# A shared 16 KB buffer, earlier gathers, a four-column-group MLP, and other engines for probability copies and low parts

## The reference

```
mod = silu(c) @ w_ada + b_ada                       # shift, scale, gate, twice
u   = rmsnorm(x) * (1 + scale1) + shift1
q_a,k_a,v_a,q_b,k_cmp,v_cmp,k_sel,v_sel,k_win,v_win,g_nsa,g_a,g_b = split(u @ w_in)
o_a   = MoBA attention: own block of 256 and the 3 best earlier blocks, 8 heads
o_cmp = attention over compressed keys: segments of 32, stride 16, through
        gelu(flat @ w1 + b1) @ w2 + b2              # the small MLP, hidden width 256
o_sel = attention over the 16 best blocks of 64;  o_win = over the last 512 positions
o_b   = g0*o_cmp + g1*o_sel + g2*o_win
x = x + gate1 * ((sigmoid(g_a)*(o_a @ w_pa) + sigmoid(g_b)*(o_b @ w_pb)) @ w_out)
h = rmsnorm(x) * (1 + scale2) + shift2
a, b = split(h @ w_gu);  x = x + gate2 * ((silu(a)*b) @ w_down);  y = rmsnorm(x)
```

## Time and profile before

| what | value |
|---|---|
| median of 3 runs | 1269.82 us (1265.07 to 1272.02) |
| profiled execution | 1268.64 us, span 1266.2 us |
| mean granted TensorE clock | 0.926 |
| busy: TensorE, VectorE, ScalarE, GpSimd | 1133.7, 550.6, 511.7, 310.2 us |
| bytes moved by DMA | 219.94 MB, mean 174 GB/s |

### The profile page before, as it was taken

How to read it: one execution, slowest core, us unless ns; L and a number is a source line. 1 busy time by engine, 2 the same in 40 slices (tenths; PEclk the granted TensorE clock), 3 DMA queues, 4 the chain that set the end, 5 groups by cost and what they waited for, 6 DMA issues and landing times. The chain is left out here.

```text
span 1266.2 us, 24086 instructions
## 1 busy us (share of the span) xinstructions
PE 1133.7 (90%) x8797; PEld 952.6 (75%) x8797; DVE 550.6 (43%) x1009; ACT 511.7 (40%) x942; POOL 310.2 (25%) x112
## 2 busy tenths in 40 slices
PE   7899978759899999999898989969997799997996
PEld 3678955637686767777776868668997699997995
DVE  2400043432726354453628272636345577775004
ACT  3321231524544635454546354443542344332221
POOL 1233400001010000000000100044574176665540
PEclk9789987769999999999899999978998799998997
DMA  9788754028374564646373836394563054444201
GB/s 335 208 306 279 258 170 181 34 99 341 110 264 151 206 199 159 221 152 239 111 278 108 291 106 216 100 270 126 158 199 121 15 191 139 149 152 164 100 0 41
DMA packets 130048, 219.94 MB, mean 174 GB/s; under 512 B 19364, under 2 KB 74145, under 8 KB 125330
## 3 DMA queue, kind: packets, MB, share of 16 engines
...
## 5 line engine op out<-in xcount | busy, mean ns | idle before, releaser
L1839 POOL TENSOR_TENSOR b_slabL<-t_slab,b_slabH 128x2048 fp32r<-128x2048 f32 (+1 forms) x53 | 227.6, 4311 | 157.0 <-ACT b_slabH L1990 157.0
L1124 POOL DMA_INDIRECT t_nsa<-cache_nsa_kv,t_index x32 | 30.1, 940 | 587.7 <-ACT t_relay L1461 346.4
L104 PE MATMUL ps<-b_uH,b_slabH 128*128 128x320 f32 x480 | 152.3, 317 | 16.5 <-DVE b_uL L2088 9.0
L105 PE MATMUL ps<-b_uL,b_slabH 128*128 128x320 f32 x480 | 151.1, 315 | 0.0
L106 PE MATMUL ps<-b_uH,b_slabL 128*128 128x320 f32 x480 | 150.2, 313 | 0.0
L1990 ACT ACTIVATE b_slabH<-t_slab 128x2048 fp32r<-128x2048 f32 (+1 forms) x53 | 94.3, 1785 | 119.8 <-PE ps L106 111.1
L1233 PE MATMUL ps<-t_XT,t_slab 128*128 128x254 f32 x512 | 121.0, 391 | 0.0
L1195 PE MATMUL ps<-t_XT,t_slab 128*128 128x254 f32 x512 | 116.1, 380 | 1.4 <-ACT t_KTr L1461 0.7
L1233 PEld LDWEIGHTS ps<-t_XT,t_slab 128*128 128x128 f32 x512 | 97.9, 196 | 20.7 <-issue 8.6
L104 PEld LDWEIGHTS ps<-b_uH,b_slabH 128*128 128x128 f32 x480 | 92.4, 192 | 18.9 <-issue 16.2
L1195 PEld LDWEIGHTS ps<-t_XT,t_slab 128*128 128x128 f32 x512 | 94.8, 190 | 13.5 <-DVE t_XT L1445 2.0
...
## 6 DMA issues: line engine op xcount, KB each, us to landing
...
```

The lines of the kernel that those rows point to most:

```text
L104: pe.matmul(out, w_high, x_high, start=start, stop=False, **kw)
L105: pe.matmul(out, w_high, x_low, start=False, stop=False, **kw)
L1124: pool.indirect_dma_start(out=nsa[:, q % 2, :], out_offset=None, in_=d["cache_nsa_kv"], in_offset=bass.IndirectOffsetOnAxis(ap=t["index"][ ...
L1839: pool.tensor_tensor(slabL[:, s, 0:values], slab[:, s, 0:values], slabH[:, s, 0:values].bitcast(F32), ALU.subtract).then_inc(w_split, 1)
```

## The change

One buffer `nsa` of 16 KB per partition is allocated for the whole program. In the front it takes two slabs of w_ada, in the prompt the segments, then the first two gathers of the decode part, in the last decode turn u, and in the back part u and the gates. The first two gathers are issued in the prompt, after the segment transposes. The wait for the spill of the prompt's outputs moves into the decode part. The MLP's hidden layer is spread over four groups of 32 output rows, each with a quarter of the accumulation, and the matmuls that follow (with `fold`, a matrix with ones at every 32nd row) both transpose and add the four groups. In the prompt ScalarE makes all copies of transposed probabilities. In the back part VectorE makes the low parts, at written-out places of its list, and the first slab and u are split in halves and pairs. The core of the diff:

```diff
     rows_p, rows_s = t["rows_p"], t["rows_s"]
-    ada_slab = [slab[:, s, :] for s in range(SLOTS)] + [rows_p[:, :, :].rearrange("p i c -> p (i c)")[:, 0:SLABW],
-                                                        t["cp"][:, 0:SLABW]]
...
+def gather_segments(pool, t, d, b, q):
+    pool.indirect_dma_start(out=t["nsa"][:, q % 2, :], out_offset=None, in_=d["cache_nsa_kv"],
+                            in_offset=bass.IndirectOffsetOnAxis(ap=t["index"][:, b:b + 1], axis=0),
+                            element_offset=q * 2048).then_inc(t["nsa_landed"][q % 2], 16)
+
+
 UNITS = [(br, qt) for br in (0, 2, 3) for qt in range(2)]
...
+    pt_tr, pt_act, pv_mm, pv_taken = (sem("p_pt_tr"), sem("p_pt_act"), sem("p_pv_mm"),
                                               sem("p_pv_taken"))
-    dve_step, spilled = sem("p_dve_step"), sem("p_spilled")
...
-            sp.wait_ge(spilled, 64)
+
+        @block.gpsimd
+        def _(pool):
+
+            pool.wait_ge(seg_tr, 1)
+            for q in range(2):
+                gather_segments(pool, t, d, 0, q)
...
+                    pe.wait_ge(pt_act, job - 1)
                 return ps[4 + job % 2]
...
                 done = first_job[u] + jobs_of[u]
-                pe.wait_ge(pt_dve, done // 2)
-                pe.wait_ge(pt_act, done // 2)
+                pe.wait_ge(pt_act, done)
                 if u:
...
                 pe.wait_ge(w1_landed, 16 * 5)
-                pe.wait_ge(segs_done, 5)
+                pe.wait_ge(segs_done, 6)
                 for w in range(2):
-                    for part in range(2):
-                        for lp in range(8):
-                            last = pe.matmul(ps[7][0:PC1, 256 * w:256 * w + 256], XT[:, w, part, lp, :],
-                                             w1[:, w, 8 * part + lp, :], start=part == 0 and lp == 0,
-                                             stop=part == 1 and lp == 7)
+                    for i in range(4):
+                        for g in range(4):
+                            part, lp = divmod(4 * i + g, 8)
+                            last = pe.matmul(ps[7][32 * g:32 * g + 32, 256 * w:256 * w + 256], XT[:, w, part, lp, :],
+                                             w1[:, w, 8 * part + lp, :], start=i == 0, stop=i == 3)
                 last.then_inc(conv_mm, 1)
             def hidden_transposes():
                 pe.wait_ge(hidn_done, 1)
                 for c in range(4):
-                    last = pe.transpose(ps[7][:, 32 * c:32 * c + PC1], hidn[:, P * c:P * c + P], ident[0:PC1, 0:PC1])
+                    last = pe.matmul(ps[7][:, 32 * c:32 * c + 32], hidn[:, P * c:P * c + P], t["fold"][:, :],
+                                     start=True, stop=True)
                 last.then_inc(hid_tr, 1)
...
                 act.wait_ge(conv_mm, 1)
-                act.activation(hidn[:, :], ps[7][0:PC1, :], ACT.Copy).then_inc(hidn_done, 1)
+                act.activation(hidn[:, :], ps[7][:, :], ACT.Copy).then_inc(hidn_done, 1)
...
-                for j in (1, 3):
+                for j in range(4):
                     pt_copy(first_cmp_job + j)
...
             for u, (br, qt) in enumerate(UNITS):
-                for job in range(first_job[u] + 1, first_job[u] + jobs_of[u], 2):
+                for job in range(first_job[u], first_job[u] + jobs_of[u]):
...
         def _(dve):
             steps = Steps(dve, dve_step)
-
-            def pt_copy(job):
-                dve.wait_ge(pt_tr, job + 1)
-                dve.tensor_copy(pt_dst(job), ps[4 + job % 2][0:pt_rows(job), :]).then_inc(pt_dve, 1)
...
-
-            between = [segment_copies, hidden_bias, None, compressed_scores, compressed_outputs, None]
+            between = [segment_copies, hidden_bias, None, compressed_scores, compressed_probs, None]
             biased(0)
             biased(1)
             for u in range(NU):
                 normed(u)
                 if u + 2 < NU:
                     biased(u + 2)
-                for job in range(first_job[u], first_job[u] + jobs_of[u], 2):
-                    pt_copy(job)
                 if between[u]:
...
                     load_quarter(it, 3, Kr, 0, 512, k_landed[0])
+                    sp.wait_ge(kept, NB * 4)
+                    sp.wait_ge(relaid, NB * 8)
+                    sp.wait_ge(filled, nth(NB - 2, ("sel", 3, 0)))
+                    sp.dma_start(nsa[:, :, :].rearrange("p a b -> p (a b)")[:, 0:KT * TOK], d["spill_u"]).then_inc(t["u_back"], 16)
             for q in range(2):
                 load_k(0, q)
+            sp.wait_ge(t["o_spilled"], 64)
             load_window(0)
             for q in range(3):
...
         def _(pool):
-            def gather(b, q):
-                pool.indirect_dma_start(out=nsa[:, q % 2, :], out_offset=None, in_=d["cache_nsa_kv"],
-                                        in_offset=bass.IndirectOffsetOnAxis(ap=t["index"][:, b:b + 1], axis=0),
-                                        element_offset=q * 2048).then_inc(nsa_landed[q % 2], 16)
-
...
-            gather(0, 0)
-            gather(0, 1)
             for b in range(NB):
                 for q in range(4):
                     after = (b, q + 2) if q < 2 else (b + 1, q - 2)
                     if after[0] < NB:
                         slot_free(b, q)
-                        gather(*after)
+                        gather_segments(pool, t, d, *after)
...
             act.wait_ge(zeroed, 3)
+            act.wait_ge(t["o_spilled"], 64)
             stage_queries(0)
...
                 assert steps.n == DVE_STEPS, steps.n
+            dve.wait_ge(t["o_spilled"], 64)
...
-            for n in range(2):
-                sp.dma_start(uT[:, 4 * n:4 * n + 4, :].rearrange("p k n -> p (k n)"),
-                             d["spill_u"][:, 4 * n * TOK:(4 * n + 4) * TOK]).then_inc(u_back[n], 16)
-            sp.dma_start(ex, d["c_expand"]).then_inc(exp_landed, 16)
             for br in range(4):
                 sp.dma_start(oT[:, br, :, 0:SEQ],
                              d["spill_o"][:, br * 4 * SEQ:(br + 1) * 4 * SEQ].rearrange("p (g t) -> p g t", g=4))\
                     .then_inc(o_back, 16)
+            sp.wait_ge(o_whole, 4)
+            sp.dma_start(ex, d["c_expand"]).then_inc(exp_landed, 16)
...
-            def low_part(n, it, values=SLABW):
-                s = n % SLOTS
-                pool.wait_ge(w_high, it * 4 + n + 1)
-                pool.tensor_tensor(slabL[:, s, 0:values], slab[:, s, 0:values], slabH[:, s, 0:values].bitcast(F32),
-                                   ALU.subtract).then_inc(w_split, 1)
-
             pool.sem_inc(w_split, OPEN)
             for br in range(4):
                 pool.tensor_copy(oT[:, br, :, SEQ:TOK], t["oT_s"][:, br, :, :]).then_inc(o_whole, 1)
-            with pool.Fori(0, 4) as it:
-                for i in range(4):
-                    low_part(i, it, SLABW if i < 2 else HALF)
-            with pool.Fori(4, N_END // 4) as it:
-                for i in range(4):
-                    low_part(i, it)
-            for n in range(N_END // 4 * 4, N_END):
-                low_part(n, 0)
-
         @block.tensor
         def _(pe):
...
-                split(i, it)
+                if not isinstance(it, int) or i:
+                    split(i, it)
                 for m in range(2):
...
-                        if i == m == 0 and k % 4 == 0:
-                            pe.wait_ge(u_split, k // 4 + 1)
+                        if isinstance(it, int) and i == m == 0 and k % 2 == 0:
+                            pe.wait_ge(u_split, k // 2 + 1)
+                            if k == 4:
+                                split(i, it)
                         high, low = {0: (uH, uL), 1: (uH, uL), 2: (oH, oL), 3: (bH, bL)}[i]
                         last = split_matmul(pe, bank[:, 0:TOK], *weights(i, 256 * k + P * m), high[:, k, :],
...
-            high_mix(0, 0)
-            for n in range(2):
-                act.wait_ge(u_back[n], 16)
-                act.activation(uH[:, 4 * n:4 * n + 4, :], uT[:, 4 * n:4 * n + 4, :], ACT.Copy).then_inc(u_high, 1)
+            act.wait_ge(slab_landed[0], 16)
+            act.wait_ge(u_back, 16)
+            for n in range(4):
+                if n < 2:
+                    c = slice(HALF * n, HALF * n + HALF)
+                    act.activation(slabH[:, 0, c], slab[:, 0, c], ACT.Copy).then_inc(w_high if n else u_high, 1)
+                pair = slice(2 * n, 2 * n + 2)
+                act.activation(uH[:, pair, :], uT[:, pair, :], ACT.Copy).then_inc(u_high, 1)
             for i in range(1, 4):
...
-            for n in range(2):
-                dve.wait_ge(u_high, n + 1)
-                half = slice(4 * n, 4 * n + 4)
-                dve.tensor_tensor(uL[:, half, :], uT[:, half, :], uH[:, half, :], ALU.subtract).then_inc(u_split, 1)
+
+            def low_part(n, it, values=SLABW):
+                s = n % SLOTS
+                dve.wait_ge(w_high, it * 4 + n + 1)
```

(53 more changed lines are left out.)

46 lines of the change are left out of this document (24 added, 22 removed).

## The result

| kernel | median us (lowest to highest) | ratio to the kernel before, 95% interval |
|---|---|---|
| before, 4 runs | 1269.34 (1265.07 to 1272.02) | |
| changed, 4 runs | 1226.23 (1223.91 to 1231.04) | 0.967 [0.963, 0.971] |

The forecast was 1226; the saving is 43.1 us by the medians. The profiled execution of the changed kernel was the longest of its four, 1231.04 us (span 1229.1), so the two spans differ by 37.1 only. 1.9 us of what is missing are in the front, where the first score matmul came at 174.5 us before and at 176.4 after; it lies between 172.4 and 176.9 in the profiled executions of this study.

A forecast was written before the change was run, and what follows sets the result against it. TensorE, busy nine tenths of the span, was taken as the bound, so only its waits counted. Savings of 16.1 (prompt), 5.5 (gathers) and 21.8 (back), 43.4 in all, took 1268.64 to 1225.2, stated as 1226 us; range 1218 to 1241.

The forecast's parts named there:

- MLP: Prompt: matmuls in four column groups side by side take 6.5 us instead of 16.03; 9.5 saved, bounds 7.4 and 11.7.
- Copies: Prompt: ScalarE makes all probability copies, so exponentials of units 3 and 5 start with the maximum; 6.6 us saved.
- Gathers: Decode part's start: first gathers issued in the prompt, so ScalarE need not wait for rows; 5.5 us saved, bounds 4.0 and 7.0.
- Start of the back part: u lands during the last decode turn and TensorE starts 3.3 us into the block; 4.7 us saved.
- w_out: Output projection: VectorE's z subtractions run undisturbed by GpSimd; 6.0 us of wait and 2.4 of half clock, 8.4 saved.
- Down: Before the down projection: the 6.7 us wait goes, with some 2.0 of half clock after it; 8.7 saved.
- Gate/up: Gate/up loop: VectorE busy 27 of 50 us with low parts, covered by TensorE's matmuls; 0 saved.
- Rival E: Back part: VectorE, in order, becomes the pace, 62 us on top of the forecast, 1288 us; chance 0.03.
- A: Prompt: ScalarE sets the pace and the clock stays at half; 8.7 us less gained, 1235 us; chance 0.14.
- B: Back part: VectorE's long instructions are its own, not GpSimd's doing, so both waits stay; 1248 us; chance 0.07.
- C: One prefetch, the gathers or u, is not hidden; 5 us less gained, 1231 us; chance 0.07.
- D: Everything at its better bound: copies 7.7, MLP 11.7, gathers 7.0, both back places; 1219 us; chance 0.05.

The follow-up runs named there:

- three_undone: Changed kernel with VectorE making every second probability copy, first gathers issued at the decode part's start and u loaded at the back part's start: 1238.89 us.
- copies_shared: Changed kernel with VectorE making every second copy of transposed probabilities again: 1229.17 us.
- mlp_one_group: Changed kernel with the MLP's matmuls back in one column group of 31 columns: 1236.63 us.
- gathers_late: Changed kernel with the first two gathers issued at the start of the decode part again: 1227.48 us.
- gpsimd_dummies: Changed kernel with useless GpSimd subtractions, memsets and copies issued when VectorE's low parts begin: 1226.56 us.

## Why the prediction was right, and where its terms were not

The total came out to a fraction of a microsecond because terms that were too large and too small met, not because each was right. That closeness is luck: the four runs alone span 7.1 us. What was right is more than the number: each place that the prediction named did give time, by the mechanism it gave.

- **MLP, predicted 9.5.** M fell by 10.0, and undoing it cost 10.4. Right in size, by two errors that nearly cancel. The price was too high: time multiplied by granted clock gives 3.5 us at full clock (5.9 us at 0.59 here, 5.1 us at 0.68 in three_undone), where the estimate had 4.3. And the clock was lower than forecast: 0.63 from 202 us to the end, where full clock was expected.
- **Copies, predicted 6.6.** The mechanism was right: both exponentials start at the maximum. At its place the term was right in size too: from the MLP's last matmul to the first exponential of unit 5 it is 32.4 us in copies_shared and 25.1 to 26.4 in the changed kernel and the kernels with its prompt and no fillers, 6.0 to 7.3 less.
- **Gathers, predicted 5.5.** At its place the term held: from the end of the last outputs to the relay the changed kernel takes 4.5 us instead of 10.5, 4.0 by the early gathers and 2.0 by the moved wait. The step that failed is "nothing but the staging is behind it": the staging, and with it the relay, stands behind VectorE's set-up, and that behind the moved wait for the spill, so 2.6 us of that wait stay on the path. Some 1.2 of the gain went to half clock in the matmuls behind. Against the mean, P grew by 4.3 with the gathers late. Copies, gathers and moved wait together: 12.1 predicted, 96.2 - 86.8 = 9.4 measured.
- **Start of the back part, predicted 4.7.** The wait fell from 9.0 to 4.3: 4.7, and the first split matmul comes 3.5 us into the part as forecast. But 1.1 of it belongs to the low parts and not to u: with VectorE making them in the kernel before, the wait was 7.9. U was 3.6 longer in this execution, by half clock in the first slab and above all in the gates' expansions (10.6 us for 8.3 to 8.9); in four others of the same code (mlp_one_group, gathers_late, copies_shared, gpsimd_dummies) U was 27.6 or 27.7.
- **w_out, predicted 8.4.** Z fell by 9.3: 6.1 of wait and 3.2 in the matmuls. Forecast were 6.0 and 2.4. In four of nine executions with this back part Z was 32.1, with the clock at 0.71 to 0.86 for some 8 us, so there it fell by 7.7.
- **Down, predicted 8.7.** W fell by 9.1; the wait of 6.7 is gone entirely. Low parts as a whole: 17.1 predicted, 16.6 when undone, 17.2 and 18.4 by the stages.
- **Gate/up, predicted 0.** The stretch from the last w_out matmul to the first down matmul took 172.6 and 172.4 us. VectorE was busy 23.9 of 50 us (27 estimated). Rival E had no ground.
- **Rivals.** A had the clock of the MLP nearly right and the copies wrong: ScalarE stood idle before both exponentials. B was excluded by two kernels. C did not occur, both prefetches were hidden. D's better bounds were reached by the down projection alone; the MLP (10.0 of 11.7) and w_out (9.3 of 10.5) lay between forecast and bound.

The sum by undone parts is 10.4 + 16.6 + 12.7 = 39.7 of 43.1; by the intervals of the ratios each time is uncertain by 3 to 5 us. Why the clock falls at one moment of the decode turns and not at another was not settled: no run here holds the code's moment fixed.
